# Where a piece of the state stands in VectorE's list between the evictions of a chunked delta-rule kernel

## The reference

```python
sol = lax.linalg.triangular_solve(a_mat + eye, rhs, left_side=True, lower=True,
                                  unit_diagonal=True)
u, w = sol[..., :dv], sol[..., dv:]
...
def step(s, inp):
    u_n, w_n, qk_n, qd_n, kt_n, gt_n = inp
    v_new = u_n - jnp.einsum("bhck,bhkv->bhcv", w_n, s)
    o = jnp.einsum("bhck,bhkv->bhcv", qd_n, s) + jnp.einsum("bhcj,bhjv->bhcv", qk_n, v_new)
    s = s * gt_n[..., None, None] + jnp.einsum("bhck,bhcv->bhkv", kt_n, v_new)
    return s, o
```

## Time and profile before

| | |
|---|---|
| Median of 3 runs | 2920.55 us |
| Range of the 3 runs | 2913.73 to 2926.36 us |
| The profiled execution's own time | 2910.79 us |
| Its span, first to last instruction | 2909.1 us |
| Mean granted TensorE clock | 0.946 of full |
| Busy in the span | PE 90%, PEld 87%, DVE 62%, ACT 43%, POOL 41% |

### The profile page before, as it was taken

The page is one execution under the profiler, slowest core; times in us unless marked ns, Lnnn a source line. Parts: engine busy times, 40 slices in busy tenths (PEclk is TensorE's granted clock), DMA queues, the critical chain, the costliest instruction groups (busy, mean ns, idle before and its releaser), DMA issues. The chain is left out here.

```text
span 2909.1 us, 52298 instructions
## 1 busy us (share of the span) xinstructions
PE 2609.5 (90%) x18311; PEld 2517.7 (87%) x18311; DVE 1791.8 (62%) x2718; ACT 1261.8 (43%) x2180; POOL 1183.6 (41%) x1103
## 2 busy tenths in 40 slices
PE   3999999965996699999999699999998999994995
PEld 3999999965993699999999699998998999984994
DVE  5377777664005488878888667766676677764003
ACT  4466655652104244444434345454554545543002
POOL 4344443313220255444445354554554555543220
PEclk7999999987998799999999899999998999997997
DMA  4111121104103354455555442424424243214113
GB/s 149 44 58 58 59 64 58 51 30 176 43 29 121 71 159 137 128 144 142 145 150 159 144 134 51 114 50 112 107 54 111 51 114 114 60 34 168 44 36 117
DMA packets 244798, 275.48 MB, mean 95 GB/s; under 512 B 86907, under 2 KB 210380, under 8 KB 242972
## 3 DMA queue, kind: packets, MB, share of 16 engines
q1 hardware_dynamic: 240028, 256.31, 31.0%
q10 hardware_dynamic: 4608, 17.04, 1.5%
HBM read 185.78 MB, written 87.53 MB: 94 GB/s over the span
## 5 line engine op out<-in xcount | busy, mean ns | idle before, releaser
L623 PE MATMUL ps<-dn_yhi,dn_whi 128*128 128x416 f32 (+1 forms) x1152 | 395.2, 343 | 10.4 <-ACT p_vrow L1517 5.3
L2011 ACT ACTIVATE zz<-ps 104x416 fp32r<-104x416 f32 x560 | 283.8, 516 | 237.5 <-PE ps L1895 235.7
L624 PE MATMUL ps<-dn_ylo,dn_whi 128*128 128x416 f32 (+1 forms) x1152 | 376.2, 327 | 0.0
L625 PE MATMUL ps<-dn_yhi,dn_wlo 128*128 128x416 f32 (+1 forms) x1152 | 375.8, 326 | 0.0
L2103 DVE TENSOR_TENSOR pp<-ps,level_mask 104x416 fp32r<-104x416 f32 x480 | 276.1, 587 | 132.3 <-PE ps L1895 130.7
L1897 PE MATMUL ps<-pp,zz 104*104 104x208 f32 x1440 | 266.7, 295 | 25.2 <-DVE pp L2103 16.7
L623 PE MATMUL ps<-rg_yhi,rg_whi 128*128 128x416 f32 (+1 forms) x768 | 250.7, 326 | 32.0 <-PEq L80 32.0
L624 PE MATMUL ps<-rg_ylo,rg_whi 128*128 128x416 f32 (+1 forms) x768 | 251.1, 327 | 0.0
L625 PE MATMUL ps<-rg_yhi,rg_wlo 128*128 128x416 f32 (+1 forms) x768 | 250.2, 326 | 0.0
L1897 PE MATMUL ps<-zz,pp 104*104 104x208 f32 x1440 | 247.0, 282 | 0.0
L623 PEld LDWEIGHTS ps<-dn_yhi,dn_whi 128*128 128x128 f32 x1152 | 218.8, 190 | 17.4 <-issue 15.6
(11 more groups left out here) (300 smaller groups left out, 7238.0 us busy)
## 6 DMA issues: line engine op xcount, KB each, us to landing
c_nq<-nq_scratch SPq DMA_DIRECT2D x160, 169.0 KB
dn_raw<-in_dn_w_in SPq DMA_DIRECT2D x48, 512.0 KB, 4.3
qd<-rows_scratch SPq DMA_DIRECT2D x160, 104.0 KB, 3.3
rg_raw<-in_rg_w_in SPq DMA_DIRECT2D x32, 512.0 KB, 4.5
nq_scratch<-p_nq SPq DMA_DIRECT2D x48, 338.0 KB
p_ex<-rows_scratch SPq DMA_DIRECT2D x32, 422.5 KB
nq_scratch<-p_rn SPq DMA_DIRECT2D x32, 338.0 KB
o_scratch<-a SPq DMA_DIRECT2D x16, 520.0 KB, 2.8
```

The lines of the kernel that those rows point to most:

```text
L623: e.matmul(o, whi, mhi[:, t0:t0 + tn], start=(first and k == 0), stop=False)
L624: e.matmul(o, whi, mlo[:, t0:t0 + tn], start=False, stop=False)
L625: ins = e.matmul(o, wlo, mhi[:, t0:t0 + tn], start=False, stop=(last and k == end))
L2011: e.activation(zz[:, b, :, :], ps[0:CH, 2 * b + 1, 0:m4], ACT.Copy).then_inc(zev.sem, 1)
```

## The change

The work of every engine stays the same, and the lists of TensorE, ScalarE, GpSimd and SP stay as they are. In VectorE's list, the piece of slot `l` (0 to 7) goes from behind the two evictions of its own slot to between the two evictions of slot `l + 1`. The piece of slot 8 stays at the slot's end. `pre` (which issues `twos`) and `final` (which issues the scaling) keep their place behind the second eviction of their slot, so they now come ahead of that slot's piece.

```diff
+        def piece(p, l, steps, state):
+            lo, hi = steps
+            g = 2 * p - 2 + PIECES_AT[l][0] if l in PIECES_AT else -1
+            if lo <= g < hi:
+                state(g, PIECES_AT[l][1])
+
+        def period(p, steps, pre, inverse, state, finish, final, between=False):
...
                 for g in (2 * p, 2 * p + 1):
                     if lo <= g < hi:
                         inverse(g, l + 1)
+                    if between and l and g == 2 * p:
+                        piece(p, l - 1, steps, state)
                 for g in (2 * p + 2, 2 * p + 3):
                     if lo <= g < hi:
                         pre(g, l)
-                if l in PIECES_AT:
-                    g = 2 * p - 2 + PIECES_AT[l][0]
-                    if lo <= g < hi:
-                        state(g, PIECES_AT[l][1])
+                if not between or l == SLOTS - 1:
+                    piece(p, l, steps, state)
...
-                return pre, inverse, state, nothing, final
+                return pre, inverse, state, nothing, final, True
```

More of the change, by code:

```diff
@@ L1702, in both @@
             return v[:, a:b + 1:b - a] if a < b else v[:, a:(b - 1 if b else None):b - a]
-        def period(p, steps, pre, inverse, state, finish, final):
+        def piece(p, l, steps, state):
[4 more added lines that the diff above has]
+        def period(p, steps, pre, inverse, state, finish, final, between=False):
             lo, hi = steps
```

## The result

The changed kernel took 2943.16 us in the median of four runs (2940.68 to 2945.86), before 2922.38 us: a ratio of 1.0075 with an interval of 1.005 to 1.0101. It is slower, by 21 to 29 us; 31 were predicted.

What follows compares the result with a forecast made beforehand. TensorE's list was taken to bound the kernel, its waits adding one for one. Terms of 23.4, 3.5, 3.9 and 0.3 us sum to 31.1, on before's median of 2920.55 giving 2951.7 us; range 2938 to 2978.

Steps and rivals of the forecast that it cites:

- That TensorE sets the pace: Chunk stream: TensorE's list bounds the time, and whatever it has to wait for adds one for one.
- Slot 6, the main term: Slot 6: late `rr` starts L1967 0.73 us later in 32 periods, 23.4 us; 3.5 us more in 7 others.
- the rival without overlap: New junctions: VectorE's eviction and `rr` go strictly one behind the other; 52.7 us, so 2973 us; chance 0.07.
- The periods with scaling: Slot 6 in 7 periods: scaling also precedes `rr`; bounds 0 and 0.83 us, 0.5 taken, 3.5 us.
- Slot 5: Slot 5: addition to `c_vo` behind the first eviction makes L1954 0.26 us late in 15 periods, 3.9 us.
- 15 waits of L1954 named for the addition: Slot 5: the profile would show L1954 waiting for the addition to `c_vo` 15 times, 0.2 to 0.3 us each.
- Slots 1 and 2: Slots 1 and 2: the wait moves to the second step's products, 0.02 us late in 16 periods, 0.3 us.
- Both `st` at nothing: Slots 3 and 7: moving `st` costs nothing; if uncovered, 70 places at up to 0.33 would cost 23 us.
- The sum: All terms: 23.4 + 3.5 + 3.9 + 0.3 = 31.1 us added, 1.1% slower.
- The clock: Rival: new waits drop TensorE's clock in more periods; two more stretches give 2962 us, six 2982 us; chance 0.12.

Runs made afterwards that it cites:

- run 3: Kernel of before with only `rr` of slot 5 moved, between the evictions of slot 6; ratio to before 1.0092.
- run 5: Kernel of before with only `rr` of slot 5 moved, behind both evictions of slot 6; 2978.70 us, ratio to before 1.0205.
- run 8: Changed kernel with TensorE's sum of squares of slot 6 ahead of L1967 instead of behind it; 2932.39 us, ratio to before 1.0049.
- run 4: Changed kernel's moves for slots 0, 3, 4 and 7 only, `rr` of slot 5 back behind its own slot; ratio to before 1.0009.
- run 11: Kernel of before with only `rr` of slot 0 moved, between the evictions of slot 1; one time, 2905.82 us.
- run 6: Kernel of before with only `rr` of slot 0 moved, behind both evictions of slot 1; ratio to before 0.999.
- run 10: Kernel of before with only both `st` (slots 3 and 7) moved, between the next slot's evictions; one time, 2912.86 us.
- run 2: The changed kernel again, unchanged, beside more runs of before; 2944.44 us, ratio to before 1.0099.
- run 7: Before with `rr` of slot 0 behind slot 1's evictions, a head group's last `c_vo` addition behind the next slot 0's, tables behind slot 4; ratio 1.000.
- run 9: Kernel of before with `rr` of slot 0 behind both evictions of slot 1 and the tables behind slot 4; 2892.69 us, ratio to before 0.992.
- run 1: The kernel of before again, unchanged; ratio 1.001.

## Why the prediction was right

**That TensorE sets the pace.** Right. Outside the periods with scaling, runs 3 and 5 turn a later `rr` into time one for one, and run 8 takes it back by putting TensorE's own work into the gap.

**Slot 6, the main term.** Predicted 0.73 us in 32 periods and 0.5 in 7. Measured 0.74 in period 14, named 39 times in 39 periods, and 25 us for this move alone (run 3) against 26.9. By periods of run 3 it is 0.74 to 0.85 (once 0.9) outside the periods with scaling, and 0.1 in them. The instructions did overlap at the new junction (`rr` 0.51 behind the eviction's start), so the rival without overlap is out.

**The periods with scaling.** The mechanism was there and its size was not: 0.5 was taken out of bounds of 0 and 0.83, and 0.1 is what is left. The first part of the reasoning is wrong. The eviction of slot 6 was not held by the scaling: in period 7 it starts at 1842.86, 0.25 behind its product. I had let the Exp's end of the earlier trace rows decide when the scaling could start; in the changed kernel the scaling of slot 5 is through before the Exp of that moment has ended, so it needed an earlier one. L1973 follows at 1844.54, 1.93 after the Y product as in period 14, 0.74 late. From the Y product to L1932's first matmul it is 1840.30 - 1837.99 = 2.31 us in the earlier trace rows, and 2.89 here, 0.58 more. To slot 8's first product it is 4.99 before and 5.20 here:

```profile
1842.98 0.53 PE L1897 MATMUL ps<-uu,pp 104*104 104x208 f32 x3
```

```profile
1842.61 0.21 PE L1901 MATMUL ps<-pp,zz 104*104 104x104 f32 x1
...
1844.54 1.12 PE L1973 MATMUL ps<-rr,tb 104*104 104x128 f32 x8 [0.58 <-DVE rr L2131]
1845.50 1.63 PE L1938 MATMUL ps<-pp,c_nq 104*104 104x104 f32 x16
...
1847.81 0.54 PE L1903 MATMUL ps<-uu,pp 104*104 104x208 f32 x3
```

The first line is before, the others are the changed kernel. So 0.21 of the 0.74 is left there, and 0.10 at the first L1987 behind them. What takes the rest back is what the prediction named, L2109. Before, it starts at 1842.35, 4.36 behind the Y product, and slot 8's products follow 0.04 behind the end of its first instruction. In the changed kernel it starts 4.11 behind the Y product, so it is not late, and that wait is gone.

**Slot 5.** The wait is there and was taken too small: predicted 0.26 in 15 periods, measured 0.4 (run 4). From the Y product's matmul to L1954 it was 1.21 us in the earlier trace rows; the changed kernel has the addition end at 2018.80 and L1960 at 2018.94, by the 0.14 that the earlier trace rows gave, and L1954 is 0.28 later in its period. The prediction stopped there. The square on ScalarE and the evictions behind it add 0.14. The sign that it gave, 15 waits of L1954 named for the addition, did not come as it was put: the profile has the 15 waits, on the weight loads and under another name.

**Slots 1 and 2.** Right: the wait was passed from the even step to the odd one (run 11), and the gain of 0.46 did not come. It comes when `rr` lets both evictions go ahead, and then not in periods 18, 28 and 33 (run 6).

**Both `st` at nothing.** Wrong in the periods with tables. I named L1987 and L1988 as the cover of the second eviction of slot 8 and forgot what stands behind that eviction in VectorE's own list: the scaling, six instructions of tables, and the next slot's first eviction, already late. There the 0.33 is not covered, and run 10 has 0.3, and 1.0 in period 3. In all other periods away from the edges of the loop it was covered.

**The sum.** By places and runs it reads like this:

| Term | Predicted | Measured per place | Comes to |
|---|---|---|---|
| Slot 6, 32 periods | 23.4 | about 0.8 (run 3) | 25 |
| Slot 6 with scaling, 7 | 3.5 | 0.1 (run 3) | 1 |
| Slot 5, 15 | 3.9 | 0.4 (run 4) | 6 |
| Slots 1 and 2, 16 | 0.3 | 0.03 to 0.12 (run 11) | 1 |
| Both `st`, 8 periods with tables | 0 | 0.3, once 1.0 (run 10) | 3 |

That is 36 us against 31.1. The stream grew by 30.2, since periods 0, 13 and 23 of the changed kernel came out 0.2 to 0.6 us shorter than before's and not longer, and since period 39 lies outside it. So the mechanism and the main term are right, and that the total hits within 1 us is partly luck: one term too large, four too small and the edges of the loop cancel.

**The clock.** The rival did not come about at this size. In the periods away from the edges of the loop, before has one stretch at half clock, and each of the two profiles of the changed kernel has one too, at varying places. Over all runs the changed kernel loses no more to the clock than before (run 2 in the table).

```profile
2105.00:2116.00 11.00, 10.92 (x64) 10.76 (x63) 4.84 (x13) 4.08 (x10) 5.39 (x7) 0.53 1.00 278
```

This is period 18 of the changed kernel, as in the earlier trace rows; in run 2 that period stayed at full. Run 3, with the same wait for `rr`, has two such stretches. The rival became real in run 5, at twice the wait, and in run 7, with six stretches each. What decides in which of the equal periods it falls stays open.

**From the profile to the median.** The sum was 31.1 us, the stream grew by 30.2, and the medians by 20.8 and 28.8. The weak point was that before's three runs carried a spread of 13 us, and I took their median as if it were firm.

## What to carry to other kernels

A list that an engine works off in order should put first what is ready first, not what is wanted by the busiest engine's next instruction: `rr` was ready 0.34 us ahead of the eviction put in front of it, and had 0.15 us of slack. Where two consumers compete for one engine, compute for both orders when each consumer starts; if only the waiting one changes, nothing is gained (run 11). The third order may be the good one, but follow it to the next slot: in run 6 it gained in one kind of period and lost in another. And when something is costed at nothing because the next reader is far, look also at what stands behind it on its own engine and, over a semaphore, in a third engine's list (runs 4, 7 and 10). A total that fits does not show that its terms do: compare them place by place. And where runs of one kernel differ, look at their granted clocks before explaining a few microseconds.

## What the runs showed of the hardware

Tiny VectorE instructions without a PSUM operand (the copies and `head_eg` of the tables) took 0.17 to 0.18 us with GpSimd idle (run 9, period 8) and 0.63 to 0.68 us beside GpSimd's work, in the same kernel stage (every second one in period 8 of before, all four in period 8 of run 6): the tables 0.72 us in run 9 and 3.51 us in period 8 of run 6. In that period each of the slow ones ends 0.03 to 0.04 us behind the end of one of GpSimd's instructions, so each seems to wait for it; that was read off the timelines and not tried by itself. The evictions from PSUM kept their 0.58 to 0.59 us. In the unchanged kernel the tables took 2.5 us in eight of ten periods and 3.6 in two (both profiles, periods 3, 8, 18, 28 and 33), so this contention comes out in two ways without any change of the program.

TensorE's clock was at full in ordinary periods with a named wait of 0.56 us (the changed kernel) and in most with one of 1.34 us (run 5, 24.80 us at 1.00). From period 2 on and away from the edges of the loop it went to 0.51 to 0.53 of full, its 1.2 GHz level, for 3.5 to 10.5 us at a time. Behind a wait of 1.8 to 1.9 us for the tables that happened in six of seven cases (not in period 33 of run 1). Behind one of 0.7 to 1.2 us it happened in five of the other 37 (periods 8, 18, 28 and 33 of all profiles that leave the tables in their place), among them period 18 of before and of the changed kernel. Behind a wait of 1.8 us for ScalarE's evictions it happened in six of seven periods (run 7), and behind the one of 1.34 us for `rr` in periods 4 and 34 of run 5. So a longer wait made it more likely, but no length of a wait tells the cases apart here. With the tables moved (run 9) the clock did not go down there.
